# A hybrid decoder layer on one core: first-half projections as two 256-column products, copied out by ScalarE, with the sample work in another order

## The reference

```python
p = einsum('btd,de->bte', rmsnorm(x, g_pre), w_in)      # 64 column tiles of 128, plus 16 gate columns
q_a, k_a, v_a, z_a, qkv_b, z_b, beta_in, a_in = split(p)
o_a = dilated_window_attention(rope(q_a), rope(k_a), v_a)     # sample tokens: 3 windows of cached keys
o_b, S_new = gated_delta_rule(silu(conv(qkv_b)), beta, decay, S0)
y = x + rmsnorm(concat(o_a * silu(z_a), o_b * silu(z_b)) @ w_out, g_post)
```

## Time and profile before

| | us |
|---|---|
| three runs | 1201.79, 1207.5, 1209.22 |
| median | 1207.5 |
| the profiled execution | 1208.47 |
| its span, first to last instruction | 1206.6 |
| PE busy | 1150.7 (95%) |
| DVE busy | 826.4 (68%) |
| ACT busy | 472.2 (39%) |
| POOL busy | 289.2 (24%) |

### The profile page before, as it was taken

The page is one execution under the profiler, slowest core; times in us unless marked ns, Lnnn a source line. Parts: engine busy times, 40 slices in busy tenths (PEclk is TensorE's granted clock), DMA queues, the critical chain, the costliest instruction groups (busy, mean ns, idle before and its releaser), DMA issues.

```text
span 1206.6 us, 24778 instructions
## 1 busy us (share of the span) xinstructions
PE 1150.7 (95%) x8241; PEld 1067.3 (88%) x8241; DVE 826.4 (68%) x2226; ACT 472.2 (39%) x1208; POOL 289.2 (24%) x259
## 2 busy tenths in 40 slices
PE   4999999999999999999989998999899989999997
PEld 4899989988998899889978998899898979999996
DVE  4577567767776777677867786778676866565544
ACT  6453335334443444244324432453244335331211
POOL 0223112311331123122312231223122312222211
PEclk8999999999999999999999999999999999999999
DMA  7332545254535353535353534343535374423253
GB/s 249 100 110 87 168 143 184 83 170 137 179 93 183 117 185 96 180 109 183 110 166 111 180 110 166 116 177 111 164 116 176 111 251 136 149 88 93 81 211 142
DMA packets 86634, 172.63 MB, mean 143 GB/s; under 512 B 14033, under 2 KB 24114, under 8 KB 84978
## 3 DMA queue, kind: packets, MB, share of 16 engines
q1 hardware_dynamic: 85246, 169.92, 43.4%
q10 hardware_dynamic: 1312, 1.59, 0.4%
HBM read 153.17 MB, written 17.44 MB: 141 GB/s over the span
## 4 chain that ended last, share of the span: by engine, by line
issue 47%; PE 24%; POOL 13%; DVE 5%; DMA 5%; ACT 4%; SPq 1%; POOLq 0%; DVEq 0%; ACTq 0%
POOL w_lo L1996 8%; PE PJ L654 5%; DMA kvq<-in_cache_win_k 3%; PE PJ L650 3%; PE PJ L651 3%; PE PJ L652 3%; POOL mem L2045 3%; PE PJ L655 2%; PE PJ L955 2%; PE PJ L956 2%; PE PJ L957 2%; ACT w_hi L1028 1%; ACT mem L1188 1%; DVE stat L1557 1%; DVE mem L1555 1%
## 5 line engine op out<-in xcount | busy, mean ns | idle before, releaser
L654 PE MATMUL PJ<-h,w_hi 128*128 128x512 f32 x1110 | 418.6, 413 | 1.8 <-DVE memx L1419 1.8
L1996 POOL TENSOR_TENSOR w_lo<-w_raw,w_hi 128x512 fp32r<-128x512 f32 x160 | 218.0, 1363 | 791.8 <-ACT w_hi L1028 791.7
L650 PE MATMUL PJ<-h,w_hi 128*128 128x264 f32 (+1 forms) x1216 | 359.2, 295 | 0.0
L651 PE MATMUL PJ<-h,w_hi 128*128 128x264 f32 (+1 forms) x1216 | 345.5, 284 | 0.0
L652 PE MATMUL PJ<-h,w_lo 128*128 128x264 f32 (+1 forms) x1216 | 345.2, 284 | 0.0
L655 PE MATMUL PJ<-h,w_lo 128*128 128x256 f32 x1110 | 310.9, 280 | 0.0
L654 PEld LDWEIGHTS PJ<-h,w_hi 128*128 128x128 f32 x1110 | 209.0, 188 | 45.0 <-issue 2.2
L651 PEld LDWEIGHTS PJ<-h,w_hi 128*128 128x128 f32 x1216 | 230.1, 189 | 1.5
L1028 ACT ACTIVATE w_hi<-w_raw 128x512 fp32r<-128x512 f32 x320 | 196.8, 623 | 87.1 <-PE PJ L652 79.1
L650 PEld LDWEIGHTS PJ<-h,w_hi 128*128 128x128 f32 x1216 | 229.9, 189 | 0.3
L652 PEld LDWEIGHTS PJ<-h,w_lo 128*128 128x128 f32 x1216 | 228.9, 188 | 0.0
(11 more groups left out here) (320 smaller groups left out, 1677.8 us busy)
## 6 DMA issues: line engine op xcount, KB each, us to landing
w_raw<-in_w_in SPq DMA_DIRECT2D x256, 256.0 KB, 2.7
w_raw<-in_w_out SPq DMA_DIRECT2D x64, 256.0 KB, 2.8
kvq<-in_cache_win_k SPq DMA_DIRECT2D x24, 512.0 KB, 5.2
kvq<-in_cache_win_v SPq DMA_DIRECT2D x24, 512.0 KB, 4.8
mem<-scratch_p SPq DMA_DIRECT2D x24, 512.0 KB, 6.9
out<-memx SPq DMA_DIRECT2D x16, 260.0 KB, 5.5
mem<-in_x_prompt SPq DMA_DIRECT2D x4, 1024.0 KB, 10.1
gx<-scratch_dk SPq DMA_DIRECT2D x8, 512.0 KB, 5.7
```

The source lines that it names most:

```text
L650: pe.matmul(ps, wh, h_hi[:, k, tok], start=k == 0, stop=False)
L651: pe.matmul(ps, wh, h_lo[:, k, tok], start=False, stop=False)
L654: pe.matmul(both, wh, h2[:, :, k, tok], start=k == 0, stop=False)
L1996: pool.tensor_tensor(w_lo[:, par, 4 * q:4 * q + 4, :], w_raw[:, q, :, :], w_hi[:, par, 4 * q:4 * q + 4, :].bitcast(F32), ALU.subtract).the ...
```

## The change

1. In the 63 tiles of the main loop half 0 no longer streams 512 columns: `w_hi*h_hi` and `w_hi*h_lo` are two products of 256 columns into the same 256 sums. The output projection keeps the 512 columns.
2. With one sum per token DVE's 63 reduces go. ACT copies half 0 out in step 5 of the tile, and `guard` moves to ACT with it; PE waits for `proj_sb` alone, and `proj_half` is gone.
3. The scaling of `S0` moves from POOL (one operation of 128x1024) to ACT (eight of 128x128, in two parts of four).
4. Key block 2 of a head moves from DVE's end of the head into the next head (`last_keys`, steps 9 and 11), the other two blocks one step later and in other places; SP loads key block 0 one step earlier, ahead of a weight load, and two loads of cached values two steps later. Some small pieces of the sample work move by a step.

```diff
 # PE
-                if q == 0 and not first:
-                    if half == 1 or out or isinstance(T, int) and T <= 2:
-                        pe.wait_ge(s["proj_sb"], made(T, half) - 2)
-                    else:
-                        pe.wait_ge(s["proj_half"], T - 2)
+                if q == 0 and not first:
+                    pe.wait_ge(s["proj_sb"], made(T, half) - 2)
...
-                wide = half == 0 and not (isinstance(T, int) and T < 2)
+                wide = half == 0 and out
 # ACT: copy_out counts 1 and waits for no proj_half; guard(h, j) is moved here word for word
...
                         if seg % 2 == 0:
                             hi(T + 1, j % 2, seg // 2)
+                        if seg == 5:
+                            guard(h, j)
+                            copy_out(T, 0, *DST[j])
...
                 rsqrt(dd[:, 9:11, :], MD[:, 1, 0:2 * NB].rearrange("p (a b) -> p a b", a=2), 1.0, s["d_rs"])
-                yield from idle(13)
+                yield
+                act.wait_ge(s["d_ks"], h + 1)
+                for b in range(NB):
+                    last = act.activation(S0[:, b, :], S0[:, b, :], ACT.Copy, scale=dd[:, 11, b:b + 1])
+                    if b == 3:
+                        yield
+                last.then_inc(s["S0_scaled"], 1)
+                yield from idle(11)
 # DVE
-                        if seg == 4 and not (isinstance(h, int) and h == 0 and j == 0):
-                            half_out(h, j)
...
-                yield from fused(None, q_rows, q_rows, dd[:, 1], (3, 5, 6))
+                yield from fused(None, q_rows, q_rows, dd[:, 1], (3, 6))
...
-                yield from idle(56)
+                yield from idle(57)
                 dve.wait_ge(s["qb_in"], 16 * h + 16)
-                for n in range(3):
+                for n in range(2):
                     yield from key_block(h, n)
-                    if n < 2:
-                        yield from idle((1, 3)[n])
+                    yield from idle(2)
+
+            def last_keys(hh, at, gap):
+                yield from idle(at)
+                yield from key_block(hh, 2, gap)
...
-            def attn_decode(hh, late=0, gap=32, each=2):
+            def attn_decode(hh, late=0, gap=31, each=2):
...
                 stretch(h, [tail_a(h - 1), mix_b(h), own_b(h), own_a(h), mix_q(h), delta_decode(h),
-                            attn_decode(h - 1), decode_keys(h)])
+                            last_keys(h - 1, 9, 2), attn_decode(h - 1), decode_keys(h)])
...
-            work = [later(tail_a(NH - 1)), attn_decode(NH - 1, late=-6, gap=12, each=1)]
+            work = [last_keys(NH - 1, 4, 1), later(tail_a(NH - 1)), attn_decode(NH - 1, late=-6, gap=12, each=1)]
 # SP
-            def attn_decode(hh, at=10, out=7, back=2):
+            def attn_decode(hh, at=12, out=5, back=2):
...
-                yield from idle(52)
+                yield from idle(51)
                 if not first:
                     sp.wait_ge(s["pv_ok"], h)
                 keys(0)
+                yield
                 sp.wait_ge(s["qrow_out"], 192 * h + 192)
 # POOL
-                pool.wait_ge(s["d_ks"], h + 1)
-                pool.tensor_tensor(S0[:], S0[:], dd[:, 11, :].unsqueeze(2).to_broadcast((P, NB, P)),
-                                   ALU.mult).then_inc(s["S0_scaled"], 1)
```

More of the change, by code:

```diff
@@ L333, in build @@
             "c_in ba_in g_in consts s_loaded x_sq rstd_ok x_scaled hT_ps h_hi_ok h_lo_ok st_ps st_sb memset_ok "
-            "w_hi_ok w_lo_dve w_lo_pool w_used proj_ps proj_half proj_sb "
+            "w_hi_ok w_lo_dve w_lo_pool w_used proj_ps proj_sb "
             "gates_pe gates_act gates_dve "
@@ L967, in _ @@
                     if q == 0 and j == 0:
-                        pe.wait_ge(s["proj_sb"], 2 * T_O) if half == 1 else pe.wait_ge(s["proj_half"], T_O - 2)
+                        pe.wait_ge(s["proj_sb"], 2 * T_O - 1 + half)
                     elif q == 0:
@@ L1050, in copy_out @@
             def copy_out(T, half, dst, off=0):
-                late = not (isinstance(T, int) and T < 2)
                 act.wait_ge(s["proj_ps"], made(T, half))
-                if late:
-                    act.wait_ge(s["proj_half"], T - 1)
                 o = off + half * SPLIT
@@ L1058, in copy_out, with guard @@
                 act.activation(dst[:, o:o + WIDTH[half]], PJ[0:n, bank(T, half), 0:WIDTH[half]], ACT.Copy).then_inc(
-                    s["proj_sb"], 2 if late else 1)
+                    s["proj_sb"], 1)
             def guard_first():
                 act.wait_ge(s["cw_ok"], 1)
+            def guard(h, j):
+                if j == 0:
+                    act.wait_ge(s["scores"], NC * h)
+                    act.wait_ge(s["qkp"], h)
+                    act.wait_ge(s["q_row"], 3 * h)
+                elif j in (1, 2, 4):
+                    n = min(j, 3)
+                    act.wait_ge(s["conv_ok"], 3 * h + n)
+                    act.wait_ge(s["crow_out"], 16 * (3 * h + n))
+                elif j == 3 and (not isinstance(h, int) or h > 0):
+                    act.wait_ge(s["z_ok"], h)
+                elif j == 5:
+                    act.wait_ge(s["mix_qk"], h + 1)
+                    act.wait_ge(s["dkq"], h + 1)
+                elif j == 6:
+                    act.wait_ge(s["mix_T1"], 3 * h + 2)
+                    act.wait_ge(s["d_add"], h + 1)
+                elif j == 7:
+                    act.wait_ge(s["z_ok_b"], h + 1)
             def stretch(h, before, work):
@@ L1390, in lo @@
                     s["w_lo_dve"], 1)
[L1392 to L1420, removed]
             def stretch(h, work):
@@ L1790, in delta_decode @@
                 dve.tensor_tensor(dd[:, 8, :], dd[:, 7, :], dd[:, 7, :], ALU.mult).then_inc(s["d_vec"], 1)
-                yield from idle(2)
-                yield
+                yield from idle(3)
                 dve.wait_ge(s["z_ok_b"], h + 1)
@@ L1802, in decode_keys, with key_block @@
             def decode_keys(h):
-                yield from idle(56)
+                yield from idle(57)
                 dve.wait_ge(s["qb_in"], 16 * h + 16)
-                for n in range(3):
+                for n in range(2):
                     yield from key_block(h, n)
-                    if n < 2:
-                        yield from idle((1, 3)[n])
-            def key_block(h, n):
+                    yield from idle(2)
+            def last_keys(hh, at, gap):
+                yield from idle(at)
+                yield from key_block(hh, 2, gap)
+            def key_block(h, n, gap=1):
                 dve.wait_ge(s[f"kb{n}_in"], 16 * h + 16)
@@ L1817, in key_block @@
                     if b == 3:
-                        yield
+                        yield from idle(gap)
                 last.then_inc(s["red"], 1)
-            def attn_decode(hh, late=0, gap=32, each=2):
+            def attn_decode(hh, late=0, gap=31, each=2):
                 yield from idle(13 + late)
@@ L2065, in _ @@
             pool.memset(xq[:, 0:3], 0.0).then_inc(s["cw_ok"], 1)
-            stretch(0, [own_b(0), own_a(0), mix_b(0), delta_decode(0)])
+            stretch(0, [own_b(0), own_a(0), mix_b(0)])
             with repeat(pool, 1, NH) as h:
-                stretch(h, [tail_a(h - 1), own_b(h), own_a(h), mix_b(h), delta_decode(h)])
+                stretch(h, [tail_a(h - 1), own_b(h), own_a(h), mix_b(h)])
             work = [later(tail_a(NH - 1))]
```

2 lines of the change are left out of this document (removed).

## The result

The changed kernel takes **1186.87 us** in the median of 4 runs (1186.31 to 1187.96) against 1207.88 us before (1201.79 to 1209.22): a ratio of 0.9839, 95% interval 0.981 to 0.9869, faster by 1.6%. The forecast was 1188 us. The total came out as forecast; what brought it is in part not what the forecast said, and the changed kernel is not the best use of its own idea: one of its parts alone gives 1181.9 us.

A forecast was written before the change was run, and what follows sets the result against it. The prediction took PE to be the bound, with its waits for DVE at the head's end removable. Removed waits less new costs summed to -20.2 us from the profiled 1208.5 us, giving 1188 us, range 1177 to 1205 us.

The forecast's parts named there:

- What bounds the kernel: Whole kernel: PE is busy 1150.7 of 1206.6 us, and its waits are for DVE, which works through its list in order.
- `rr`: Head's end, chunk chain (L884): without the reduce `rr` starts about 0.6 us earlier; PE's 5.9 us wait shrinks by 5.2 us.
- what the view leaves out: PE's waits at the head's end: each removed wait is worth 0.16 us more than shown, -3.5 us in all.
- S: Head's end, chunk chain (L874): S is ready before PE asks, so the whole wait goes, -8.3 us.
- `gB`: Next head's first scores (L764): key block 2 no longer stands ahead of `gB` on DVE, so the wait goes, -8.4 us.
- Products: Half 0 of 63 main-loop tiles: two 256-column products for one of 512 cost 0.055 us a tile, +3.5 us.
- (a): Step 11 of the next head: block 2 ends late, ahead of PE's score transposes; 0.2 us in 7 heads, +1.4 us.
- (b): Tile 2: ACT waits for the row transfer, making the scaled keys PE transposes late; 0.25 us in 7 heads, +1.8 us.
- (c): Between levels of the inverse: eight `S0` scalings on ACT, 2.6 us while ACT waits for PE, costed at nothing.
- Row transfers: Tile 2: ACT's copy takes over the 24.9 us that DVE stood waiting for the row transfers.
- Start of the output stage: PE behind DVE's low parts (L955): block 2's products move to a later gap, so 1.5 of 3.6 us go.
- ACT late in tile 2: Rival, chance 0.08: the row transfer lands late and ACT's copy delays PE, 33 us in 7 heads, giving 1221 us.

The follow-up runs named there:

- one of its parts alone: The kernel before with only DVE's list of the sample attention re-ordered (key block 2 in the next head, query a step later): 1181.93 us, ratio 0.9783.
- the control: The changed kernel run once more with no edit: 1185.39 us (1183.70 to 1187.58), ratio 0.9816.

## Why the forecast was right, and where not

- **What bounds the kernel**: right. PE's work stayed, its waits for DVE went.
- **`rr`, -5.2**: size about right (-7.2, some of which the forecast has under what the view leaves out), cause only half. "Without the reduce" is one cure, which alone takes the row from 5.9 to 1.5 us; the moved steps of DVE's sample attention do it all with the reduce in place (-6.8). I had these steps in one half sentence and did not cost them.
- **S, -8.3**: right in size (-9.6 with what the view leaves out). I gave it to three edits together; the runs show that SP's alone is enough, and that DVE's list alone is.
- **`gB`, -8.4**: right. DVE's list alone takes all of it, SP's order alone 5.5 us; with the sum gone and SP's order kept, 2.8 us of wait return when DVE's list is put back.
- **Products, +3.5**: 5.68 us for an undisturbed half, as forecast, but +2.0 in all, or +2.7 with what is left over, where 63 times 0.08 us would be 5.0. Only seven halves are undisturbed; that the others hide it in their gaps is likely and not shown.
- **(a) and (b), +1.4 and +1.8**: right, +1.2 and +1.6. (a) is in no row of the waits and shows only in the starts; it is gone when DVE's list is put back. (b) came in 3 heads by 0.5, not in 7 by 0.25.
- **(c) S0 on ACT at nothing**: this step failed. I looked at ACT's gaps between the levels of the inverse; the scalings delay a step of a sigmoid for which DVE waits, and DVE brings an addition of the inverse 0.27 us late in each head, 2.1 us in all. A gain that I did not count, 0.2 us per head at a later level, hid most of it (it is there with the products and copies alone too).
- **Row transfers**: size wrong. In tile 2 of seven heads ACT waits 8.7 us for them, not 24.9, since it reaches that place later than DVE did. The view gives 5.6 of it:

```profile
ACT memx L1053 <- DMA out<-memx: 5.6, 5, 2.7
```

In two heads it puts the wait down to PE, whose half 0 had long been done, while the copy starts 1.53 us behind the issue of the transfer, as it does in the fourth head (428.10 and 429.63). In the fifth head (timelines of SP and ACT):

```profile
545.15 0.35 SPq L481 DMA_DIRECT2D out<-memx  x1
...
546.68 0.38 ACT L1053 ACTIVATE memx<-PJ 128x256 f32<-128x256 f32 x1 [1.55 <-PE PJ L650]
```

The three longest of these waits, 1.55, 1.56 and 2.70 us, stand in the very three heads in which the scaled keys are late, as (b) has it.

- **Start of the output stage, -1.5**: the waits for DVE fell by 1.7, as forecast. That the whole came to -1.2 is chance: a new wait for ACT behind its pause took 1.4, and a stretch at half clock before gave 0.9.
- **Not foreseen**: 1.4 us in the first head, where ACT's copy stands behind a step of a sigmoid and a small operation that waits 0.86 us for DVE; the clock, +2.8 at the start and -1.4 near 985 us; the last head's 1.0 us.
- **The rivals**: none came. ACT late in tile 2 shows only as (b), and one first product of a tile waited for the copy in the last head, 0.8 us, behind the transfer of 2.70 us.

The total was right because the waits were found. That it came within about 1 us is luck: costs and gains that I missed (+8.3 and -5.0 us) partly cancel, and the terms that I had came 3.6 us better than forecast. The largest of the missed costs, the clock's 2.8 us at the start, belongs to one execution, as the control shows. By its own terms the forecast's spread began at 1181, not at 1182 us.

## What to carry over

Where several edits cure one wait, put each back and do each alone: here S and `rr` each had two cures, so undoing one showed next to nothing, and only the single edits showed that DVE's list does it all. An engine with idle time is not free: ask which instruction stands behind the added work, and who waits for that. A load is free only as long as the product beside it is as long as the load.

## What the runs showed of the hardware

- With a 128-column load for each product, 256 columns of the projection still hide it (0.118 us a product) and 128 do not: 0.11 us for each of four. Sixteen columns with such a load also take 0.11 us.
- Half clock came at different places in two executions of the same kernel (at 35 to 42 us in one, at 973 to 977 us in the other), each time after a wait of PE (1.3 us, 2.1 us). Such a stretch cost up to 2.8 us beyond the wait's own row. That the wait brings it on is not shown: in the second execution PE waited 1.5 us at 33 us, and the clock stayed at full speed.
- The query's broadcast of 512 KB took 6.3 to 6.7 us to land (medians) in the five runs that issue it 0.5 us behind the 512 KB of key block 0, and 4.7 to 5.0 us in the nine that issue it 3 us or more behind.
- ACT stood still for 1.2 to 2.7 us, once or twice in nearly every run, with no wait that the profile shows; the place moved with ACT's list.
